# The second mixer of a two-block layer: stacked S5 inputs, keys and values made once, and another order

## The reference

```python
xs, q, ckv, qi, ki, wi, ga, gb = split_cols(u @ w_in, IN_SIZES)
# S5 branch: 32 groups of 16 channels, 64 complex states each
bu_re = einsum('blgc,gpc->blgp', xg, bb_re);  bu_im = einsum('blgc,gpc->blgp', xg, bb_im)
s_re, s_im = scan over positions of  s = lambda * s + bu
y = einsum(s_re, c_re) - einsum(s_im, c_im) + d_skip * xs
y_ssm = glu(gelu(y) @ w_glu + b_glu)
# attention branch: 8 heads of 64, latent of 128, 128 keys kept per query
iscore = sum_h relu(qi_h @ ki) * wi_h ;  sel = top_k(causal iscore, 128)
logits = (q @ w_uk) / 8 @ c_kv[sel] ;  p = softmax(logits)
y_att = ((p @ c_kv[sel]) @ w_uv) @ w_attn_proj
merged = sigmoid(ga) * y_ssm + sigmoid(gb) * y_att
h = h + gate1 * (merged @ w_out)
```

## Time and profile before

| | |
|---|---|
| median of 3 runs | 1640.93 us (1637.22 to 1641.56) |
| the profiled execution | 1639.83 us |
| its span, first to last instruction | 1638.5 us |
| mean granted TensorE clock | 0.987 |
| PE busy | 1571.8 us (96%) |
| DVE busy | 850.2 us (52%) |
| ACT busy | 864.2 us (53%) |

### The profile page before, as it was taken

The page is one execution under the profiler, slowest core; times in us unless marked ns, Lnnn a source line. Parts: engine busy times, 40 slices in busy tenths (PEclk is TensorE's granted clock), DMA queues, the critical chain, the costliest instruction groups (busy, mean ns, idle before and its releaser), DMA issues.

```text
span 1638.5 us, 17633 instructions
## 1 busy us (share of the span) xinstructions
PE 1571.8 (96%) x6556; PEld 1201.6 (73%) x6556; DVE 850.2 (52%) x1700; ACT 864.2 (53%) x1091; POOL 334.1 (20%) x348
## 2 busy tenths in 40 slices
PE   6899999999999999999999878989999999999997
PEld 5687788788788888888776545546687888888886
DVE  6778634554577765445349999863465122111011
ACT  5678868744555555444444415557555444444441
POOL 2111111111111111111133335542211111111111
PEclk9999999999999999999999999999999999999999
DMA  8667787899899898998787545418696998888882
GB/s 259 156 157 190 172 201 185 207 312 315 224 244 261 200 219 215 265 249 212 170 219 187 140 124 154 116 47 278 177 232 160 239 241 188 188 194 184 189 181 77
DMA packets 93893, 324.64 MB, mean 198 GB/s; under 512 B 10464, under 2 KB 10464, under 8 KB 93552
## 3 DMA queue, kind: packets, MB, share of 16 engines
q0 software_dynamic: 37856, 137.76, 44.7%
q1 hardware_dynamic: 52128, 178.28, 32.3%
q10 hardware_dynamic: 3824, 7.47, 1.2%
HBM read 177.59 MB, written 16.78 MB: 119 GB/s over the span
## 4 chain that ended last, share of the span: by engine, by line
PE 82%; DVE 10%; ACT 4%; issue 1%; DMA 1%; POOL 1%; ACTq 0%; DVEq 0%
PE ps L664 26%; PE ps L667 25%; PE ps L665 25%; PE ps L844 1%; DVE pl_f L1899 1%; DVE sml L1896 1%; DVE pl_f L1843 1%; PE ps L950 1%; PE ps L921 1%; PE ps L738 1%; DVE pl_f L1845 1%; PE ps L706 1%; DVE pl_f L1504 1%; ACT wlo L1038 1%; ACT whi L1031 1%
## 5 line engine op out<-in xcount | busy, mean ns | idle before, releaser
L664 PE MATMUL ps<-pl_r,whi 128*128 128x512 f32 x1976 | 793.7, 402 | 25.4 <-DVE pl_f L1839 13.3
L665 PE MATMUL ps<-pl_r,wlo 128*128 128x512 f32 x1976 | 784.3, 397 | 0.0
L667 PE MATMUL ps<-pl_r,whi 128*128 128x512 f32 x1976 | 784.3, 397 | 0.0
L664 PEld LDWEIGHTS ps<-pl_r,whi 128*128 128x128 f32 x1976 | 373.6, 189 | 141.5 <-issue 27.8
L667 PEld LDWEIGHTS ps<-pl_r,whi 128*128 128x128 f32 x1976 | 373.2, 189 | 91.5 <-DVE pl_r L1436 0.9
L665 PEld LDWEIGHTS ps<-pl_r,wlo 128*128 128x128 f32 x1976 | 373.6, 189 | 87.4 <-issue 0.3
L2042 POOL DMA_DIRECT2D wlo<-raw x246 | 213.2, 871 | 1094.6 <-ACT wlo L1038 1069.2
L1031 ACT ACTIVATE whi<-raw 128x1024 fp32r<-128x1024 f32 x247 | 259.9, 1053 | 175.1 <-PE ps L667 139.1
L1038 ACT ACTIVATE wlo<-raw 128x1024 fp32r<-128x1024 f32 x246 | 257.4, 1046 | 0.0
L2016 DVE TENSOR_TENSOR pl_f<-ps,pl_f 128x512 f32<-128x512 f32 x22 | 15.2, 691 | 177.5 <-PE ps L667 177.5
L1420 DVE TENSOR_TENSOR pl_r<-pl_f,pl_r 128x512 fp32r<-128x512 f32 x112 | 77.6, 693 | 37.0 <-ACT pl_r L1058 21.0
(11 more groups left out here) (231 smaller groups left out, 1342.0 us busy)
## 6 DMA issues: line engine op xcount, KB each, us to landing
wlo<-raw POOLq DMA_DIRECT2D x246, 512.0 KB, 6.3
raw<-in_w SPq DMA_DIRECT2D x245, 512.0 KB, 5.3
pl_f<-in_mod SPq DMA_DIRECT2D x48, 512.0 KB, 7.5
tab<-pl_f SPq DMA_DIRECT2D x16, 512.0 KB, 6.7
pl_f<-tab POOLq DMA_DIRECT2D x16, 512.0 KB, 4.1
spill<-pl_f ACTq DMA_DIRECT2D x16, 256.0 KB, 2.5
pl_f<-spill SPq DMA_DIRECT2D x16, 256.0 KB, 5.0
pl_f<-in_x SPq DMA_DIRECT2D x12, 256.0 KB, 7.9
```

The lines of the kernel that those rows point to most:

```text
L664: matmul(out, wh, sr(pair, kk, "hi"), start=start, stop=False)
L665: matmul(out, wl, sr(pair, kk, "hi"), start=False, stop=False)
L667: mm = matmul(out, wh, sr(pair, kk, "lo"), start=False, stop=stop)
```

## The change

- The S5 input in fp32r. The matrices (`s5_turn`) are split on ACT and DVE into halves, and `xs` too (`xq`). SP copies them by DMA into stacks of three 32-row parts: `wst` holds hi, hi, lo, and `st` holds hi, lo, hi. One fp32r product over 96 rows then gives the sum of the three partial products. That is 12 DMAs of 128 KB ahead of the mixer, and 48 of 64 KB, 12 for each 4 steps.
- The S5 output products are issued for two steps together, real parts of both, then imaginary parts of both, in different column groups of the array.
- Keys (4 products with `w_uk`) and values (4 products with `w_uv`) are made once from the latent, with 8 copies on ACT. The per-head `latent`, the product by the latent, its copy and the product by `w_uv` go.
- Scores of two heads are issued together, each over 64 rows. The queries carry a minus sign, so that DVE takes a minimum, which is the bias of the exponential; L1943 goes.
- The exponentials are not scaled. The 8 sums of a head pair are inverted at once, spread to rows by PE (`att_rows`), copied by ACT, and DVE multiplies the output of the pair by them. The transposes stand the other way round and wait for the exponentials alone. The value products of two heads are interleaved in two column groups.
- The projection becomes a generator of its own, `a` (16 steps), and the merge is done inside `u`. `w_out_2` starts with its first four tiles interleaved.
- x (`xw`) is written to memory at the start of the mixer and read back (`xz`) in `u`; 8 tiles of 256 KB each way.
- The first three tables are loaded earlier in POOL's program.
- `ORDER` is another string, of 56 `d`, 64 `s`, 64 `g`, 16 `a` and 32 `u` that do something.

The diff, cut to its core (the removed lines are those of the code above):

```diff
--- before.py
+++ after.py
...
 ORDER = (
-    "dsgdgsgdgsgdgsgdgsgdgsgdgsgdgsgdgsgdgssgdgsgdgsgdgsgdgsgdgsgdgsgdgsgdsgdsgsdgsdgssgdsgsd"
-    "gsdgssgdsgdsgsdgsdgssgdsgdsgsdgsdgssgdsgsdgsdgssgdsgdsgsdgsdgssgdsgdsgsdgssgdsdssdsdssds"
-    "dsuuuuuuuduudududududuudududududuudududududuududududuu"
+    "dsdgdddgggsddggggsssdgggggsdggssgsgdgggsdgdgddsggsdsgggsggddgggggsdssdgsgggggsdddgdggsgggg"
+    "gsggdssgdggdgssgggsssgsdgsgsdddssgddddddgssdsggsgdsssdsdsddsdssdsssdsdddddssdssdssdsaddssd"
+    "sssaasaaaaassaaaaaauauuausuuuuuuuuuuuuuuuuuuuuuuuuuuuuu"
 )
...
+        def outputs(last):
+
+            if last % 2 == 0:
+                return
+            j, i = divmod(last, 4)
+            if i == 1:
                 take("s5_y", j)
...
+            for c, z in ((0, "q1"), (1, "q3")):
+                for s in (last - 1, last):
+                    col = 32 * (s % 4)
+                    T.wait_ge(at("z_im" if c else "z_re", s))
+                    matmul(y[col:col + 32], k.ssm_c[:, c, s, :], sb(z, s), start=c == 0, stop=c == 1,
+                           tile_position=(0, col)).then_inc(*done.tick(None, (z, s)))
             if i == 3:
...
                 b = take("bu", c, s)
-                T.wait_ge(at("xs", j), at("s5_bt", 1))
-                matmul(b, k.bt[rows, c, j, :], sb("xs", j)[rows], start=True,
-                       stop=True).then_inc(*done.tick(("bu", c, s)))
+                T.wait_ge(at("wst"), at("st", s))
+                matmul(b, k.wst[0:96, i, c, j, :], sr("st", s)[0:96], start=True,
+                       stop=True).then_inc(*done.tick(("bu", c, s), *([("st", s)] if c else [])))
                 give("bu", c, s)
...
+                    for i in range(4):
+                        b = take("k_ps", i)
+                        T.wait_ge(at("ck"), at("uk"))
+                        matmul(b, k.uk[:, 0, 128 * i:128 * i + 128], sb("ck"), start=True,
+                               stop=True).then_inc(*done.tick(("k_ps", i)))
...
+                        b = take("v_ps", q)
+                        matmul(b, sb("ck")[:, 128 * q:128 * q + 128], k.uk[:, 1, :], start=True,
+                               stop=True).then_inc(*done.tick(("v_ps", q)))
...
+        def scores(hp):
...
+                for h, hh in enumerate((2 * hp, 2 * hp + 1)):
+                    rows = slice(64 * h, 64 * h + 64)
+                    b = take("sc", hh, t)
+                    T.wait_ge(at("qt", hp), at("kt", hp))
+                    matmul(b[:, 0:128 * (t + 1)], sb("qt", hp)[rows, 128 * t:128 * t + 128],
+                           sb("kt", hp)[rows, 0:128 * (t + 1)], start=True, stop=True).then_inc(
...
+                for q in range(4):
+                    b = take("p_turn", hh, q)
+                    for t in range(q, 4):
+                        T.wait_ge(at("p_exp", hh, t))
+                        mm = transpose(b[:, 128 * t:128 * t + 128],
+                                       queries("fs", hh, t=t)[:, 128 * q:128 * q + 128], k.ident)
+                    mm.then_inc(*done.tick(("p_turn", hh, q)))
+                    give("p_turn", hh, q)
+                done.release(*[("fs", hh, i) for i in range(3)])
...
-                                   sb("fs", hh, t)[:, 128 * q:128 * q + 128], k.ident)
-                mm.then_inc(*done.tick(("p_turn", hh, t), ("fs", hh, t)))
-                give("p_turn", hh, t)
-            yield
...
+            b = take("att_rows", hp)
+            T.wait_ge(at("p_inv", hp))
+            r = sm("rsm", 8 * (hp % 2), 8).rearrange("p (h t) -> p h t", h=2)
+            for t in range(4):
+                for h in range(2):
+                    mm = matmul(b[64 * h:64 * h + 64, 128 * t:128 * t + 128],
+                                r[:, h, t:t + 1].broadcast_to([128, 64]), k.ident, start=True,
+                                stop=True, tile_position=(0, 64 * h))
+            mm.then_inc(*done.tick(("att_rows", hp)))
+            give("att_rows", hp)
+            b = take("att_ps", hp)
             for q in range(4):
...
+                for h, hh in enumerate((2 * hp, 2 * hp + 1)):
+                    T.wait_ge(at("pt", hh, q), at("vt", q))
+                    mm = matmul(b[64 * h:64 * h + 64, 128 * q:S],
+                                sb("vt", q)[:, 64 * hh:64 * hh + 64], sb("pt", hh, q)[:, 128 * q:S],
+                                start=q == 0, stop=q == 3, tile_position=(0, 64 * h))
+            mm.then_inc(*done.tick(("att_ps", hp)))
+            done.release(*[("pt", hh, q) for hh in (2 * hp, 2 * hp + 1) for q in range(4)])
+            give("att_ps", hp)
...
+                A.wait_ge(at("s5_turn", c), *freed("bt", "hi"))
+                act(sr("bt", "hi")[:, S * c:S * c + S], ps("s5_turn", c), ACT.Copy).then_inc(
...
+        if j == 0:
+            rounded("xq", 0, sb("xs", 0), ("xs", 0))
...
+                    act(f, f, ACT.Exp, bias=sm("nm", c), scale=-1.0,
+                        accum_out=sm("rsm", c)).then_inc(*done.tick(("p_exp", hh, t)))
...
+                V.wait_ge(at("bt_hi", c), *freed("bt", "lo"))
+                tt(sr("bt", "lo")[:, half], ps("s5_turn", c), sr("bt", "hi")[:, half].bitcast(F32),
+                   ALU.subtract).then_inc(*done.tick(("bt_lo", c), ("s5_turn", c)))
...
+    rest("xq", 0, sb("xs", 0))
...
+            if s % 4 == 2 and s < 14:
+                rest("xq", s // 4 + 1, sb("xs", s // 4 + 1))
...
-                    sb("fs", hh, t)[:, 0:kmax], ps("sc", hh, t)[:, 0:kmax],
-                    masks[:, masks_at[t]:masks_at[t] + kmax], 1.0, NEG, ALU.add, ALU.max,
-                    sm("mx", c)).then_inc(*done.tick(None, ("sc", hh, t)))
-                V.wait_ge(done.now())
-                ts(sm("nm", c), sm("mx", c), -1.0, None, ALU.mult).then_inc(
-                    *done.tick(("p_max", hh, t)))
...
+                    V.wait_ge(at("sc", hh, t), at("mask", t), *freed("fs", hh, 3 - t if t else 1))
+                    if hp > 1:
+                        V.wait_ge(at("p_exp", 2 * hp - 3, 0))
+                    V.eng.tensor_tensor_reduce(
+                        queries("fs", hh, t=t), ps("sc", hh, t)[:, 0:128 * (t + 1)],
+                        queries("masks", t=t), 1.0, -NEG, ALU.add, ALU.min, sm("nm", 8 * (hp % 2) + 4 * h + t)).then_inc(
...
-                kmax, c = 128 * (t + 1), 4 * (hh % 2) + t
-                V.wait_ge(at("p_inv", hh, t))
-                ts(sb("fs", hh, t)[:, 0:kmax], sb("fs", hh, t)[:, 0:kmax], sm("rsm", c), None,
-                   ALU.mult).then_inc(*done.tick(("p", hh, t)))
...
+            r = sm("rsm", 8 * (hp % 2), 8)
+            V.wait_ge(at("p_exp", 2 * hp, 0), at("p_exp", 2 * hp + 1, 0))
+            reciprocal(r, r).then_inc(*done.tick(("p_inv", hp)))
+            yield
+            yield
+            V.wait_ge(at("att_ps", hp), at("ar", hp), *freed("ao", hp))
+            tt(sb("ao", hp), ps("att_ps", hp), sb("ar", hp), ALU.mult).then_inc(
+                *done.tick(("ao", hp), ("att_ps", hp), ("ar", hp)))
+            rest("att", hp, sb("ao", hp), ("ao", hp))
...
+            yield
+            fb = sb("sg", m + 8)
+            V.wait_ge(at("sg", m + 8), at("w_attn_proj_2", m))
+            tt(fb, ps("w_attn_proj_2", m), fb, ALU.mult).then_inc(
+                *done.tick(("fb", m), ("w_attn_proj_2", m)))
...
+    def merge(m):
+        f = sb("side", m)
+        V.wait_ge(at("fb", m), at("side", m))
+        tt(f, f, sb("sg", m + 8), ALU.add).then_inc(*done.tick(("merge2", m), ("sg", m + 8)))
+        rest("mg2", m, f, ("side", m))
...
-    for m in range(8):
-        f, fb = sb("side", m), sb("sg", m + 8)
-        V.wait_ge(at("sg", m + 8), at("w_attn_proj_2", m))
-        tt(fb, ps("w_attn_proj_2", m), fb, ALU.mult).then_inc(
-            *done.tick(None, ("w_attn_proj_2", m)))
-        V.wait_ge(done.now(), at("side", m))
-        tt(f, f, fb, ALU.add).then_inc(*done.tick(("merge2", m), ("sg", m + 8)))
-        rest("mg2", m, f, ("side", m))
+    merge(7)
...
+    halves(units.ahead())
+    weights(8)
+    for s in range(3):
+        weights(8)
+        load_table(s)
...
+    Q.wait_ge(*freed("wst"), at("bt_hi", 1), at("bt_lo", 1))
+    for i in range(4):
+        for h, part in enumerate(("hi", "hi", "lo")):
+            dma(sr("wst")[32 * h:32 * h + 32, 2 * S * i:2 * S * (i + 1)].bitcast(F32),
+                sr("bt", part)[32 * i:32 * i + 32].bitcast(F32)).then_inc(
+                *k.wst_in.tick(("wst",) if i == 3 and h == 2 else None))
+    k.wst_in.release(("bt", "hi"), ("bt", "lo"))
+    weights(32)
...
+        for s in range(4 * j, 4 * j + 4):
+            i = s % 4
+            Q.wait_ge(*freed("st", s), at("xq", j, "hi"), at("xq", j, "lo"))
+            for h, part in enumerate(("hi", "lo", "hi")):
+                dma(sr("st", s)[32 * h:32 * h + 32].bitcast(F32),
+                    sr("xq", j, part)[32 * i:32 * i + 32].bitcast(F32)).then_inc(
+                    *k.st_in[s % 8].tick(("st", s) if h == 2 else None))
...
+    def s5():
+        stacks(0)
```

(44 more changed lines are left out.)

456 lines of the change are left out of this document (229 added, 227 removed).

## The result

The changed kernel takes 1625.78 us (median of 6 runs, 1624.24 to 1630.14) where the kernel before took 1637.53 beside it (1635.56 to 1641.56): a ratio of 0.9929, 95% interval 0.991 to 0.9948. It is faster, by 0.7%; forecast were 3.1%, and the time lies above the range (1612). The profiled execution has a span of 1622.9 us.

The account below looks back on a forecast made before the run. DVE's row was taken to bound the mixer until 1089 us, then PE's queue to 1196.0 instead of 1245.86, 49.9 us less; 1639.8 - 49.9 = 1590 us. Range 1573 to 1612, the forecast's own 1580 to 1598.

Parts of the forecast that it names:

- What bounds the kernel: Mixer: DVE's row with PE waiting until about 1090 us, then a queue of PE work alone to 1245.86.
- Loads and queues: SP's added DMAs: wst 4.7 us of transfer, first stack -1 to +3 us, taken as 0 since DVE is held anyway.
- With the later 12 us of waits kept: DVE's row after: first turn 843.0, work 233, waits 13 us, so the last turn back ends at 1089.
- 228 of prices and 22.6 of waits: DVE's row before, 837.19 to 1087.82: 250.6 us split into summed instruction prices of 228 and waits of 22.6.
- PE ahead of that point: PE work until 1089: 33 to 61 us saved, leaving 213 to 241 us of 246, so not the bound.
- Behind 1089: PE resumes at 1091.4, output products to 1095.0, then 80 blocks of 56.1 and w_out_2 of 44.9 us; end 1196.0.
- The rival on transfers: In the u steps, 66 us of transfers against 45 of PE bound the kernel; 1611 without buffer cover; chance 0.06.
- waits gone: DVE's 12 us of waits behind 865 all vanish, giving 1578, or 1573 with a faster clock behind; chance 0.15.
- A pair's chain: DVE waits 3 to 5 us for each of four head pairs' attention chains, giving 1604 to 1610; chance 0.15.
- The clock: Bursts of PE work between waits run at the low clock: 23 us later, 1613, smaller share 1600; chance 0.07.
- Slower by SP's queue: Each of 16 S5 steps waits some 6 us for its stack, 96 us in all, giving 1686; chance 0.03.
- It doesn't do what it says: Pairs run one after the other, fp32r costs as fp32; PE bounds ahead of 1089 by 10 us, 1600; chance 0.02.

Follow-up runs that it names:

- run with stacks and early tiles: Changed kernel with bt's slots given back behind the norm of u, first stacks issued earlier, seven modulation tiles loaded at the last g step: 1602.26 us, ratio 0.9776.
- run with early tiles: Changed kernel with seven of the twelve modulation tiles of the u steps loaded by SP at the last g step: 1619.02 us, ratio 0.9879.

## Why the prediction failed, step by step

- **What bounds the kernel**: right. DVE's row, then a queue of PE work. The chain of the sum is right, and with start and tail mended the forecast is missed by 9.2 us at the sum of squares.
- **The start, +14.5 us**: the step that failed is "Loads and queues". The forecast priced `wst` as 4.7 us of transfer and the 60 small DMAs as hidden, and gave the first stack -1 to +3 us. Measured are 8.7 us for a slot that a copy still read, which the forecast did not look for at all, and 6.9 us for the first stacks. The chain behind it was right: with both mended the first turn starts at 842.0 to 842.3, against 843.0.
- **The row, +9.0 us**: the step that failed is "With the later 12 us of waits kept". Ahead of the search the waits went about as forecast: DVE's idle time there fell from 10.5 to 2.6 us. Behind its start it was not kept: it rose from 16.5 to 21.2. New there are 4.3 us for copies of a stack and 3.5 for a rest on POOL, and the waits for POOL's adds grew from 1.8 to 3.5; the 4.7 us for a half made by ACT shrank to 2.8. So idle time fell by 3.2 us in all where I let 9.6 go, which makes 6.4 of the 9.0. In the two pairs of runs that differ by the stacks, the row is 2.5 and 4.6 us shorter without them (252.1 beside 254.6, 250.9 beside 255.5), the three rests of `xq` included; the wait for POOL's rest was not tested. The other 2.6 are prices: busy time went up by 7.6 us instead of 5, since the seven rests took 8.6 and not 4.2 us and one comparison of the first mask 2.9, while the scores took 13.7 and not 16. The split of the row before into 228 of prices and 22.6 of waits was sound: busy are 223.7, and 6.5 of the 27.0 us of idle time are gaps under 0.15 us that lie inside my prices.
- **POOL's adds**: the forecast has no such term, and they cost 17 us of the row where it was measured. Yet they are a small part of the miss. The first scans were long before the change too (a mean of 1679 ns, then 1753), and the 5.3 us for a scan step were taken from rows that hold it. New beside the adds were the rests, which lost some 4 us there; the scaling, which had stood there before (one instruction of 0.47 us took 3.43), is gone.
- **PE ahead of that point**: forecast as no bound, "213 to 241 us of 246". It is busy 213 of 252. As a total this was right, and the input products cost 12.0 us busy instead of 7.5 without harm. One term was misread: the 37 us behind 1095 are the window's length less its blocks, and PE was busy 77.1 of those 82 us, so it is 32. As a statement on slack the total was too coarse: in the run with stacks and early tiles 12 us of it lie ahead of 1000 and 29 behind, and of 21.1 us taken from DVE ahead of 1000 only 9.0 shortened the row.
- **The tail, +9.5 us**: the step that failed is "Behind 1089", which adds up PE's work and puts the transfers at nothing; PE waited 7.1 us more and had 2.4 us more busy time than with seven tiles moved. The forecast itself, 107, is what the kernel gives once its transfers are moved. The rival on transfers named the cause with a chance of 0.06; its own price was 21 us, the measured one 9.5. Neither had POOL's wait for a gate, behind which the adding DMA stands in POOL's queue.
- **The other rivals**: waits gone, no (23.7 us of idle time are left in the row, 27.0 before). A pair's chain, no: DVE waits for no output product. The clock: the granted clock fell to 0.91 in the first part, where PE has idle time, and stands at 0.96 to 0.98 behind. It has 2.4 us of the tail's miss, which go with the waits. That it costs nothing ahead is argued, not tested. Slower by SP's queue, no, though that rival looked at the right queue: it priced a wait at every step, and the cost was one at the start and 4.3 us in the row. "It doesn't do what it says", no: the 64 instructions of the output products are 18.1 us busy, where they were 36.4, so the column groups overlap.
- **Luck**: none was needed for the direction. But the tail's 107.0 to the microsecond is partly chance: the forecast has a wait of 2.5 us at its start, and the run with early tiles has none there and 3.0 us of waits further on.

What I would do in the same place: list the waits that I keep by name, with what each waits for, instead of carrying them over as one number, and then ask of every new copy and rest which slot it reads and who writes that slot next. One question would have found both the wait at the start and the two in the row.

## What to carry to other kernels

A product that saves PE some 18 us (232.0 to 214.1 busy in the row) is worth nothing where a second engine sets the time, and what it needs (copies, slots, issues) can cost more than it saves: list for each new copy who writes its source next, and count its issues at the head of the first user. Busy time can hide a loss: compare the longest and the shortest duration of one instruction in a stretch, and look at what the neighbour engine does beside the long ones. Take busy time from the windows, not from a sum of lengths, where instructions overlap. When work is packed into a stretch without gaps, add up the transfers of that stretch and what queues behind the engine that waits for them.
